# Banded attention: the reciprocals of the row sums reach all partitions through DRAM, issued by the sync engine, and no longer through transposes on TensorE

## The reference, cut to what matters

```python
s = q @ k.T * scale                      # 128 queries x 256 keys (own block and the one before), masked
m = max(s.max(-1), sink)
p = exp(s - m)
r = 1 / (p.sum(-1) + exp(sink - m))      # one number for each query and head
o = (p @ v) * r * g                      # g: the layer's gate, one number for each output column and query
x = h + o @ w_out                        # output projection and residual
```

## Time and profile before

| | us |
|---|---|
| median of 3 runs | 2601.61 (2592.71 to 2602.12) |
| profiled execution | 2593.28 |
| its span in the profile | 2591.5 |
| mean granted clock of TensorE | 0.984 |

### The profile page before, as it was taken

One profiled execution on the slowest core, in us unless ns is written; L12 is line 12 of the kernel. 1 busy time (PEld: TensorE's weight loads), 2 busy tenths in 40 slices (PEclk: granted clock), 3 DMA queues, 4 the chain that ended last, 5 costly groups with the idle time before them and its releaser, 6 DMA issues. The chain is left out here.

```text
span 2591.5 us, 38243 instructions
## 1 busy us (share of the span) xinstructions
PE 2472.0 (95%) x13514; PEld 1979.2 (76%) x13526; DVE 1651.5 (64%) x3035; ACT 1371.9 (53%) x2421; POOL 379.4 (15%) x499
## 2 busy tenths in 40 slices
PE   6999999999987999999996999999999999999999
PEld 5788489788866888888885878886666787886667
DVE  5683455687668899999986655412556546742851
ACT  3352144697346788888885733323666433323850
POOL 0221121330301311111110000000232200000430
PEclk9999999999998999999998999999999999999999
DMA  7642000001229999999987511143020321113111
GB/s 250 187 139 85 1 1 1 1 1 57 93 114 392 420 410 415 417 413 410 416 326 264 178 37 66 33 134 129 31 73 27 113 80 70 33 54 145 63 50 49
DMA packets 129293, 400.26 MB, mean 154 GB/s; under 512 B 12135, under 2 KB 62572, under 8 KB 116734
## 3 DMA queue, kind: packets, MB, share of 16 engines
q1 hardware_dynamic: 117306, 359.79, 36.8%
q0 software_dynamic: 10736, 38.30, 3.7%
q10 hardware_dynamic: 1108, 0.27, 0.0%
HBM read 347.93 MB, written 50.40 MB: 154 GB/s over the span
## 5 line engine op out<-in xcount | busy, mean ns | idle before, releaser
L3245 DVE CUSTOM_DVE_ANT_0 fox_l<-PS,fox_c 128x384 f32<-128x384 f32 (+7 forms) x124 | 90.7, 768 | 82.7 <-PE PS L3275 81.7
L3181 ACT ACTIVATE fox_l<-fox_l,stat 128x384 f32<-128x384 f32 (+7 forms) x124 | 96.6, 781 | 79.6 <-DVE stat L3245 79.1
L3192 POOL COPY pad<-stat 128x128 f32<-128x128 f32 x64 | 18.7, 293 | 587.8 <-DVE stat L3258 587.6
L479 PE MATMUL PS<-wehg,xsTh 128*128 128x512 f32 x256 | 100.7, 393 | 3.6 <-ACT xsTh L2879 2.0
L479 PE MATMUL PS<-wehu,xsTh 128*128 128x512 f32 x256 | 103.6, 405 | 0.0
L479 PE MATMUL PS<-wqkh,uTh 128*128 128x512 f32 x256 | 103.0, 402 | 0.0
L481 PE MATMUL PS<-wehu,xsTl 128*128 128x512 f32 x256 | 100.8, 394 | 0.0
L481 PE MATMUL PS<-wehg,xsTl 128*128 128x512 f32 x256 | 100.5, 392 | 0.0
L481 PE MATMUL PS<-wqkh,uTl 128*128 128x512 f32 x256 | 100.2, 391 | 0.0
L480 PE MATMUL PS<-wqk_rest,uTh 128*128 128x512 f32 x256 | 99.9, 390 | 0.0
L481 PE MATMUL PS<-wehd,aTl 128*128 128x512 f32 x248 | 96.5, 389 | 0.0
(11 more groups left out here) (626 smaller groups left out, 7558.2 us busy)
## 6 DMA issues: line engine op xcount, KB each, us to landing
we0g<-in_w_expert_gate SPq DMA_DIRECT2D x16, 2048.0 KB, 10.9
we0u<-in_w_expert_up SPq DMA_DIRECT2D x16, 2048.0 KB, 9.3
we1g<-in_w_expert_gate SPq DMA_DIRECT2D x16, 2048.0 KB, 11.2
we1u<-in_w_expert_up SPq DMA_DIRECT2D x16, 2048.0 KB, 9.8
we0d<-in_w_expert_down SPq DMA_DIRECT2D x16, 2048.0 KB, 10.3
we1d<-in_w_expert_down SPq DMA_DIRECT2D x16, 2048.0 KB, 10.5
wada_rest<-in_w_ada SPq DMA_DIRECT2D x16, 1024.0 KB, 6.6
X<-in_x SPq DMA_DIRECT2D x16, 512.0 KB, 7.9
```

Of the source, the lines that this page charges most:

```text
L479: nc.tensor.matmul(out, lh, rh, start=start, stop=False)
L3181: nc.scalar.activation(prob(p, e)[:, 0:K], prob(p, e)[:, 0:K], ACT.Exp, bias=nbm[:, u % 8:u % 8 + 1], scale=-1.0, accum_out=rsum[:, u % 16 ...
L3192: nc.gpsimd.tensor_copy(rx(p).rearrange("p (e d) -> p e d", e=2), rsum[:, at:at + 2].unsqueeze(2).to_broadcast([P, 2, HD])).then_inc(rx_re ...
L3245: nc.vector.tensor_tensor_reduce(out=prob(p, e)[:, 0:K], in0=PS[:, 2 * e:2 * e + 2, :].rearrange("p a b -> p (a b)")[:, 0:K], in1=C[:, h % ...
```

## The change

PE's two transposes, its wait for POOL's tile and POOL's copy are gone. Instead SP works in pairs of units. When the reciprocals of units 2i and 2i+1 are ready, it stores the 128x8 tile transposed to a small DRAM tensor, `rw_dram`, in elements of 4 bytes, waits until that has landed, and loads for each unit two rows of 256 numbers, each repeated over 64 partitions, into the tile `rb(w)` (two DMAs a unit, one for each half of the partitions). `rb(w)` lies where `rx(w)` lay. DVE multiplies `rb(w)` by the gate when both DMAs are in, now before it waits for the output of L4028. SP's wait before it fills `rb(w)` is for the product of unit w-2.

```diff
+        residual(0)
+        for i in range(NU // 2):
+            at = 8 * (i % 4)
+            sp.wait_ge(r_ready, 2 * i + 2)
+            sp.dma_start(env.rw_dram[i % 2, :, :].rearrange("x q -> q x"), rs[:, at:at + 8],
+                         allow_slow_non_contiguous=True).then_inc(r_saved, 16)
+            sp.wait_ge(r_saved, 16 * (i + 1))
+            for w in (2 * i, 2 * i + 1):
+                if w >= 2:
+                    sp.wait_ge(rg_done, w - 1)
+                for e in range(2):
+                    sp.dma_start(rb(w)[e * HD:(e + 1) * HD, :].rearrange("p (c q) -> p c q", c=2),
+                                 env.rw_dram[i % 2, 4 * (w % 2) + 2 * e:4 * (w % 2) + 2 * e + 2, :]
+                                 .partition_broadcast(HD)).then_inc(rb_in[w % 2], 16)
+        sp.wait_ge(t_ready, NU)
+        residual(1)
...
     def on_pool(pool):
         for u in range(NU + 5):
-            if u < NU:
-                at = 4 * (u % 8)
-                pool.wait_ge(r_ready, u + 1)
-                if u >= 2:
-                    pool.wait_ge(o_ready, u - 1)
-                nc.gpsimd.tensor_copy(rx(u).rearrange("p (c e d) -> p c e d", c=2, e=2),
-                                      rs[:, at:at + 4].rearrange("p (e c) -> p c e", e=2).unsqueeze(3)
-                                      .to_broadcast([P, 2, 2, HD])).then_inc(rx_ready, 1)
...
             if w >= 0:
-                dve.wait_ge(o_ready, w + 1)
+                dve.wait_ge(rb_in[w % 2], 32 * (w // 2 + 1))
                 if w % T == 0:
                     dve.wait_ge(g_in[w // T], 16)
-                do(nc.vector.tensor_tensor(rg(w), PS[:, 6 + w % 2, 2 * P:4 * P].rearrange("p (c q) -> p c q", c=2),
-                                           block_of(g, w), ALU.mult))
+                nc.vector.tensor_tensor(rg(w), rb(w).rearrange("p (c q) -> p c q", c=2), block_of(g, w), ALU.mult
+                                        ).then_inc(rg_done, 1)
+                dve.wait_ge(rg_done, w + 1)
+                dve.wait_ge(o_ready, w + 1)
...
             if w >= 0:
                 j, b = units[w]
-                pe.wait_ge(rx_ready, w + 1)
                 if w >= 2:
                     pe.wait_ge(o_out, w - 1)
-                for c in range(2):
-                    nc.tensor.transpose(PS[:, 6 + w % 2, (2 + c) * P:(3 + c) * P], rx(w)[:, c * P:(c + 1) * P], env.ident)
                 pe.wait_ge(pt_ready, w + 1)
```

More of the change, by code:

```diff
@@ L3818, in window_steps @@
     s_ready, nb_ready, exp_done, r_ready = sem("win_s"), sem("win_nb"), sem("win_exp"), sem("win_r")
-    t_ready, pt_ready, o_ready, rx_ready, o_out = (sem("win_t"), sem("win_pt"), sem("win_o"), sem("win_rx"),
+    t_ready, pt_ready, o_ready, r_saved, rb_in, o_out = (sem("win_t"), sem("win_pt"), sem("win_o"), sem("win_rs"), [sem(f"win_rb{i}") for i in range(2)],
                                                    sem("win_oo"))
-    o_hi, o_lo, dve_step = sem("o_hi_b"), sem("o_lo_b"), sem("win_dve")
+    o_hi, o_lo, dve_step, rg_done = sem("o_hi_b"), sem("o_lo_b"), sem("win_dve"), sem("win_rg")
     wo, wl = [x[0] for x in env.wo_b], [m.rest(f"wo_b{n}") for n in range(2)]
@@ L3837, in four, with rb @@
         return PS[:, 2 * (u % 2):2 * (u % 2) + 2, :].rearrange("p a (i k) -> p (a i) k", i=2)
-    def rx(w):
+    def rb(w):
         return env.pad[w % 2][:, 2 * P:4 * P]
@@ L3870, in on_sp, with residual @@
         load(sp, env.wo_b)
-        for n in range(2):
-            if n:
-                sp.wait_ge(t_ready, NU)
+        def residual(n):
             for t in range(T):
                 sp.dma_start(H[n][:, t, :], env.ha_dram[t * P:(t + 1) * P, cols(n)]).then_inc(h_in[n], 16)
+        residual(0)
[14 more added lines that the diff above has]
+        residual(1)
         for u in range(2 * T):
@@ L4151, in build_program @@
     env.g_dram = nc.dram_tensor("g_dram", (D, S), F32, kind="Internal").ap()
+    env.rw_dram = nc.dram_tensor("rw_dram", (2, 8, P), F32, kind="Internal").ap()
     env.ha_dram = nc.dram_tensor("ha_dram", (S, D), F32, kind="Internal").ap()
```

## The result

The changed kernel takes 2695.1 us (median of 4 runs, 2692.36 to 2700.0), the kernel before 2597.72 (4 runs): a ratio of 1.0378, 95% interval 1.0349 to 1.0406. Forecast was 2614.3 us with a range to 2632. The direction was right and the size wrong: +97 us, not +13. The profiled execution took 2694.93 us, 101.7 over that of before.

A forecast was written before the change was run, and what follows sets the result against it. PE's own instructions were taken to bound the changed stage. First stall +15.8, lowered clock +2.2 and removed transposes -5.3 gave +12.7 us, put on the median 2601.6: 2614.3 us, range 2603 to 2632.

The forecast's parts named there:

- The first stall: At the stage's start, first store queues behind loads, so PE waits before unit 2's L4028: +15.8 us (14 to 19).
- The clock: After PE's idle at the stage's start, 4.5 us at half clock: +2.2 us (1 to 2.5).
- What goes: PE's 64 transposes, 0.22 us a step, removed from the stage's steps: -5.3 us, steps of 3.64 us.
- The store alone: Landing time of the 1024-element store of 4 bytes each, by itself: 3.5 us, ends 2 and 6.5.
- So nothing is paid: Pairs after the first: reciprocals return within three steps (10.9 us), slack 3.4 us, so later stores cost nothing.
- Rival A: Store takes 8 us or more; 15 later pairs each pay 1.1, first stall grows 4.5: +34, 2635 us; chance 0.15.
- B: First store doesn't stand behind the weights' loads: smaller first stall of 9.3 us, +6.2, 2607.8 us; chance 0.10.
- C: Saving absent because DVE or ACT takes over each step: +18 us, 2619.6 us; chance 0.08.
- D: PE's hole before L4028 goes too, 4.3 us more gained: +8.4 us, within 0.5%; chance 0.06.

The follow-up runs named there:

- flat store: Changed kernel, but the 128x8 reciprocal tile stored as it lies, 128 runs of 32 bytes, so reciprocals reach wrong queries: 2608.39 us, ratio 1.005.
- spread runs: SP's weight and residual loads issued one piece behind each pair: against the kernel before 0.998 with 32-byte-run store (2590.9 us); changed kernel's own store 2680.09 us.
- turned store with 8 bytes: Changed kernel, store in its transposed order but elements 8 bytes apart, loads reading another tensor so values are wrong: 2620.67 us.

## Why the prediction was wrong

**The first stall: right in kind, 15.8 us forecast.** PE's wait is 15.43 us with the flat store and 22.62 in the changed kernel. Of the difference 4.9 us are the store's own: the first one lands 9.2 us after its issue when flat, and SP goes on after 14.1 with the turned one, at 2415.84 in place of my 2410.2. That it stands behind the loads is shown by the flat run, in which a store takes 2.1 us otherwise. The spread runs take away this queue and SP's late issue together, and the long stall with them.

**The clock: right in kind.** In the flat run it is at half speed for 2.7 us after the stall (0.50 to 2415.0, 0.96 in the next us), not 4.5. In the changed kernel half speed came back after most of the later waits too, which I had not counted, since I had one stall.

**What goes: right.** 5.3 us forecast, 5.7 measured (1.8 to 9.6), steps of 3.64 us.

**The store alone: the term that was mis-sized.** "I take 3.5, nearer to the first, which has the queue and the number of runs; ends 2 and 6.5." It was 9.9 us. The row that I went by was a load with runs of 16 bytes, and that of the upper end a load too; neither writes single elements to DRAM. I priced a store by what loads with as many runs took. The 3.5 us is nearly right for 1024 elements that each have 64 bytes to themselves (3.2 and 4.1). The dear case is many short writes packed closely, of which no row of the trace before had an example, and my upper end claimed a bound that the rows couldn't give.

**"So nothing is paid": the step that failed with it, and that hid a second error.** I reckoned only the way from a reciprocal to its product against three steps. By that rule a store is free up to 6.9 us, and one of 9.9 costs 9.9 + 4.0 - 10.9 = 3.0 us a pair, 45 us in all. Measured were 77.9 us over the 15 pairs from unit 2 on, 5.2 a pair. What the rule left out is the pace of SP's own list, in which a store and the four issues behind it don't overlap: 12.64 us for each pair, where a pair took 6.8 before in the mean of these 15 (102.5 us). Over the 14 distances between stores that makes 81 us, near the measured. The turned store with 8 bytes shows the error by itself: at 5.3 us it is free by my rule, and PE waits 10.2 us for it. And the run with ACT's store shows that SP's list is not the only such bound: without it the loads meet a store, land late, and the time stays. Why they do is open.

**Rival A was the right mechanism with too small a chance and price** (0.15, 2635 us). It had the waits in each pair and the larger first stall, but the price of a pair by the same rule. B and C fell: the first store does wait behind the loads, and the gain is there. D's further 4.3 us would make 9.6 in all, the edge of the interval; it would not bring the time near the measured one. The rule of the Trainium skill that I named for A ("DMA: Bandwidth & Descriptors", section "Specifications") puts the line at 512 bytes. Whether such writes are done as read-modify-write no run here shows. Size under 512 bytes alone isn't dear in the runs: 128 writes of 32 bytes landed in 2.1 us and single elements 64 bytes apart in 3.2.

The range ended at 2632, below even A's price for a store of 8 us, though no row bounded the store from above. That "slower" came true is in good part luck: with a store as fast as I had it, the flat run is 0.5% above before, and what made the change clearly slower is the term that I had put at nothing.

## What to carry to other kernels

A transposing DMA store in elements of 4 bytes can cost far more than its 4 KB: here 9.9 us packed, 3.2 with 64 bytes to each element, and what is loaded beside the packed one can come late too. Turning the tile on PE first gave right values and the time of before. Elements set apart were only stored: those runs read other data back, so what the loads of such elements cost is untested. Where a DMA round trip is put into a pipeline, reckon its period (all that one queue must do in order for one turn) as well as its latency. A dependent small transfer goes ahead of bulk loads in its queue's list, or the first one waits for them: here for 15 us or more.

## What the runs showed of the hardware that I had not expected

A 4 KB store took 9.9 us, of which its data needed less than 3: the DMA engines then stood idle until it landed. The same 1024 elements took 3.2, 5.3 or 9.9 us with 64, 8 or 4 bytes from one to the next in the turned order, and 16.8 to 19.8 with 4 bytes between elements and 4 KB or more between the eight rows. Loads of 64 KB that land in 3.2 us in the median took up to 11.4 beside such a store issued on another queue.
